# Layer norms kept in PSUM, other PSUM banks for three projections and four turns, small steps and transfers spread, in a two-network transformer kernel

## The reference, cut to what matters

```python
for l in range(DEPTH):                       # first network, block1
    x = x + 0.5 * swiglu(rmsnorm(x, ffn1_norm[l]), w_ffn1_in[l], w_ffn1_out[l])
    u = rmsnorm(x, mix_norm[l])
    # three branches: latent attention (c_q, c_kv), a gated recurrence whose lower bounds
    # come from a softmax over hg_lower_bounds, and attention to a memory (w_mem_kv)
    x = x + merged @ w_out[l]
    x = x + 0.5 * swiglu(rmsnorm(x, ffn2_norm[l]), w_ffn2_in[l], w_ffn2_out[l])
x = rmsnorm(x, final_norm)
for l in range(DEPTH):                       # second network, block2
    x = _layer_norm(DN_ALPHA * x + 0.5 * _swiglu(x, ffn1_w1[l], ffn1_w2[l]), ln1_g[l], ln1_b[l])
    mix = _token_mix(x, w_in[l], ...)        # branches nsa (with a bias table), swa, fox
    x = _layer_norm(DN_ALPHA * x + mix, ln2_g[l], ln2_b[l])
    x = _layer_norm(DN_ALPHA * x + 0.5 * _swiglu(x, ffn2_w1[l], ffn2_w2[l]), ln3_g[l], ln3_b[l])

def _layer_norm(x, g, b):
    mu = mean(x); var = mean(square(x - mu))
    return (x - mu) * rsqrt(var + LN_EPS) * g + b
```

## Time and profile before

| | |
|---|---|
| median of three runs | 2748.06 us (2747.74 to 2748.56) |
| the profiled execution | 2751.27 us, of it 2749.5 us from the first to the last instruction |
| granted clock of TensorE, mean | 0.994 |
| PE, PEld busy | 98%, 90% |
| DVE, ACT, POOL busy | 31%, 47%, 74% |
| DMA | 474.66 MB, 173 GB/s on average |

### The profile page before, as it was taken

One profiled execution on the slowest core, in us unless ns is written; L12 is line 12 of the kernel. 1 busy time (PEld: TensorE's weight loads), 2 busy tenths in 40 slices (PEclk: granted clock), 3 DMA queues, 4 the chain that ended last, 5 costly groups with the idle time before them and its releaser, 6 DMA issues. The chain is left out here.

```text
span 2749.5 us, 46223 instructions
## 1 busy us (share of the span) xinstructions
PE 2695.5 (98%) x18758; PEld 2483.4 (90%) x18758; DVE 856.2 (31%) x1483; ACT 1283.7 (47%) x1868; POOL 2038.7 (74%) x906
## 2 busy tenths in 40 slices
PE   8999999999999999999999999999999999999998
PEld 6999899899898989989989899998988989999798
DVE  2543354111225245321211323632131132263212
ACT  4454555444444455444444444644444443464443
POOL 7888466888887845788798774368879877436886
PEclk9999999999999999999999999999999999999999
DMA  6556534555665543755565554245546555424554
GB/s 231 184 192 204 172 116 135 194 185 177 213 191 175 196 158 115 184 184 186 175 210 184 173 177 158 85 162 183 185 168 211 188 172 177 148 88 157 184 187 142
DMA packets 128731, 474.66 MB, mean 173 GB/s; under 512 B 14432, under 2 KB 14432, under 8 KB 127520
## 3 DMA queue, kind: packets, MB, share of 16 engines
q1 hardware_dynamic: 124704, 454.09, 49.5%
q0 software_dynamic: 3840, 17.81, 2.3%
HBM read 469.22 MB, written 2.62 MB: 172 GB/s over the span
## 5 line engine op out<-in xcount | busy, mean ns | idle before, releaser
L1021 POOL TENSOR_TENSOR rest<-ring,upper 128x1024 fp32r<-128x1024 f32 (+1 forms) x834 | 1998.8, 2416 | 648.2 <-ACT upper L1799 629.2
L1799 ACT ACTIVATE upper<-ring 128x1024 fp32r<-128x1024 f32 (+1 forms) x834 | 869.0, 1053 | 784.3 <-DMA ring<-in_weights 783.5
L372 PE MATMUL psA<-xT_upper,upper 128*128 128x256 f32 x2832 | 395.8, 282 | 4.5 <-DVE Sc L1695 2.4
L372 PE MATMUL psA<-xT_rest,upper 128*128 128x256 f32 x2832 | 397.4, 283 | 0.0
L372 PE MATMUL psA<-xT_upper,rest 128*128 128x256 f32 x2832 | 390.1, 280 | 0.0
L372 PEld LDWEIGHTS psA<-xT_upper,upper 128*128 128x128 f32 x2832 | 370.0, 189 | 18.8 <-ACT arena L1799 3.5
L372 PEld LDWEIGHTS psA<-xT_rest,upper 128*128 128x128 f32 x2832 | 365.3, 192 | 0.0
L1261 DVE TENSOR_TENSOR psA<-sil,psA 128x256 f32<-128x256 f32 x144 | 61.8, 429 | 958.8 <-ACT sil L1799 958.8
L372 PEld LDWEIGHTS psA<-xT_upper,rest 128*128 128x128 f32 x2832 | 358.7, 189 | 0.0
L372 PE MATMUL psY<-upper,hT_upper 128*128 128x512 f32 x704 | 204.7, 396 | 3.4 <-DVE hT_rest L1263 3.4
L372 PE MATMUL psY<-upper,hT_rest 128*128 128x512 f32 x704 | 205.8, 397 | 0.0
(11 more groups left out here) (264 smaller groups left out, 3194.1 us busy)
## 6 DMA issues: line engine op xcount, KB each, us to landing
ring<-in_weights SPq DMA_DIRECT2D x862, 512.0 KB, 3.4
G<-in_rows POOLq DMA_DIRECT2D x6, 1024.0 KB, 7.7
G<-in_rows POOLq DMA_DIRECT2D x7, 512.0 KB, 6.2
arena<-rel_by_distance POOLq DMA_DIRECT2D x8, 256.0 KB, 11.9
x<-in_x SPq DMA_DIRECT2D x2, 512.0 KB, 5.9
par<-in_params POOLq DMA_DIRECT2D x4, 256.0 KB, 6.0
xn<-in_mem POOLq DMA_DIRECT2D x1, 1024.0 KB, 10.8
memory_transposed<-arena POOLq DMA_DIRECT2D x1, 1024.0 KB, 5.7
```

Source lines behind the costliest of these rows:

```text
L372: i = pe.matmul(out, lhsT, rhs, start=start, stop=stop)
L1021: pool.tensor_tensor(rest[:, r, 0:n], ring[:, r, 0:n], upper[:, r, 0:n], ALU.subtract)\
L1799: act.activation(out, in_, func, **kw).then_inc(*up)
```

## The change

- **Layer norms in PSUM.** The half sums plus `x` stay in the Y bank instead of going to `x`; ACT squares the two banks one after the other (two operations of 512 for one of 1024); DVE subtracts the mean and multiplies by the gain in place, bank by bank, each behind ACT's square of it; the two sums of squares are added by a new small `tensor_tensor`; the last operation reads the bank and writes `x`. A Y bank is given back only then. POOL no longer waits for `x` between its power and its splits.
- **Banks.** `mk` goes to Y0 and Y1; the latents of tile 1 turn into Y0 and Y1; `kc vc` and `kb` go to Y1. `vf` of tile 0 is copied before the splits up to piece 72.
- **Bounds.** The ten operations of step 15 are spread over steps 11, 13, 15, 17 and 18 (two each) and the last one goes from 18 to 21; ACT's exponential goes from step 14 to 7 and its logarithm from 17 to 20.
- **Bias transfers.** After each second one of the eight POOL splits one piece.

```diff
+        def scaled(norm, tt, h):
+            return taken(("y", norm, 2 * tt + h)) if is_layer_norm(norm) else sig["scaled"].after(("norm", norm, tt, h))
...
-                by_features("mk", 2, rhs=memory_parts)
+                by_features("mk", 2, rhs=memory_parts, into=["Y0", "Y1"])
...
-                    turn("T0", ("cT", t, 0), [cn[:, t, j * P:(j + 1) * P] for j in range(3)])
-                    turn("T1", ("cT", t, 1), [cn[:, t, j * P:(j + 1) * P] for j in range(3, 5)])
+                    turn("TY"[t] + "0", ("cT", t, 0), [cn[:, t, j * P:(j + 1) * P] for j in range(3)])
+                    turn("TY"[t] + "1", ("cT", t, 1), [cn[:, t, j * P:(j + 1) * P] for j in range(3, 5)])
...
-                by_features("kc vc", 1)
+                by_features("kc vc", 1, into=["Y1"])
...
-                by_parts(fill(pe, next_a(), lab)[:, 0:S], s, filled(lab))
+                by_parts(fill(pe, "Y1", lab)[:, 0:S], s, filled(lab))
...
                     norm_power(norm, tt)
-                    for h in range(2):
-                        pool.wait_ge(*sig["scaled"].after(("norm", norm, tt, h)))
+                    if not is_layer_norm(norm):
+                        for h in range(2):
+                            pool.wait_ge(*scaled(norm, tt, h))
...
-                    for p in range(0, P, COPIES):
+                    for n, p in enumerate(range(0, P, COPIES)):
                         pool.dma_start(BIAS[p:p + COPIES], ...
+                        if n % 2:
+                            upto(after_mix() - MERGED + 1 + n // 2)
...
-                    add_sums(norm, tt)
-                    for b in (2 * tt, 2 * tt + 1):
-                        dve.wait_ge(*taken(("y", norm, b)))
+                    for h in range(2):
+                        lab = ("y", norm, 2 * tt + h)
+                        dve.wait_ge(*full(lab))
+                        stt_(at(lab), at(lab), 0.5, x[:, tt, 512 * h:512 * h + 512], ALU.mult, ALU.add,
+                             accum_out=st[:, 20 + 2 * tt + h:21 + 2 * tt + h]).then_inc(*sig["residual added"].up(lab))
+                    dve.wait_ge(*sig["residual added"].after(("y", norm, 2 * tt + 1)))
...
+                    def gained(h):
+                        y = at(("y", norm, 2 * tt + h))
+                        dve.wait_ge(*sig["square sum"].after(("norm", norm, tt, h)))
+                        stt_(y, y, st[:, 26 + tt:27 + tt], lnr[:, 0, 512 * h:512 * h + 512], ALU.add, ALU.mult)\
+                            .then_inc(*sig["vector step"].up())
...
-                    stt_(xn[:, tt, :], x[:, tt, :], st[:, 26 + tt:27 + tt], lnr[:, 0, :], ALU.add, ALU.mult)\
-                        .then_inc(*sig["vector step"].up())
-                    dve.wait_ge(*sig["square sum"].after(("norm", norm, tt)))
-                    ts_(st[:, tt:tt + 1], st[:, 16 + 2 * tt:17 + 2 * tt], 1.0 / D, 1e-5, ALU.mult, ALU.add)\
+                    gained(0)
+                    dve.wait_ge(*sig["square sum"].after(("norm", norm, tt, 1)))
+                    link(tt_(st[:, tt:tt + 1], st[:, 16 + 2 * tt:17 + 2 * tt], st[:, 17 + 2 * tt:18 + 2 * tt], ALU.add))
+                    ts_(st[:, tt:tt + 1], st[:, tt:tt + 1], 1.0 / D, 1e-5, ALU.mult, ALU.add)\
                         .then_inc(*sig["variance"].up(("norm", norm, tt)))
+                    gained(1)
...
-                        stt_(x[:, tt, c], xn[:, tt, c], st[:, 8 + tt:9 + tt], lnr[:, 1, c], ALU.mult, ALU.add)\
-                            .then_inc(*sig["scaled"].up(("norm", norm, tt, h)))
+                        stt_(x[:, tt, c], at(lab), st[:, 8 + tt:9 + tt], lnr[:, 1, c], ALU.mult, ALU.add)\
+                            .then_inc(*read(lab))
...
-                also = {5: lambda: bounds(l, 0), 15: lambda: bounds(l, 1), 18: lambda: bounds(l, 2)}
+                also = {5: lambda: bounds(l, 0), 11: lambda: bounds(l, 1), 13: lambda: bounds(l, 2), 15: lambda: bounds(l, 3),
+                        17: lambda: bounds(l, 4), 18: lambda: bounds(l, 5), 21: lambda: bounds(l, 6)}
...
-                    act.activation(other_junk[:, tt, :], x[:, tt, :], ACT.Square, bias=st[:, 26 + tt:27 + tt],
-                                   accum_out=st[:, 16 + 2 * tt:17 + 2 * tt]).then_inc(*sig["square sum"].up(("norm", norm, tt)))
+                    for h in range(2):
+                        act.activation(other_junk[:, tt, 512 * h:512 * h + 512], at(("y", norm, 2 * tt + h)), ACT.Square,
+                                       bias=st[:, 26 + tt:27 + tt], accum_out=st[:, 16 + 2 * tt + h:17 + 2 * tt + h])\
+                            .then_inc(*sig["square sum"].up(("norm", norm, tt, h)))
...
-                also = {14: lambda: bounds(0), 17: lambda: bounds(1)}
+                also = {7: lambda: bounds(0), 20: lambda: bounds(1)}
...
-                for t in range(TT):
-                    copy(("vf", t), VF[:, t, :], piece=69)
+                copy(("vf", 0), VF[:, 0, :])
+                copy(("vf", 1), VF[:, 1, :], piece=69)
```

More of the change, by code:

```diff
@@ L434, in turn_half @@
                     turn(f"T{h}", ("norm", norm, tt, h), [src[:, tt, (4 * h + q) * P:(4 * h + q + 1) * P] for q in range(4)],
-                         sig["scaled"].after(("norm", norm, tt, h)))
+                         scaled(norm, tt, h))
             def wait_half(norm, tt):
@@ L508, in features, with by_features @@
                                filled(lab) if j == 1 and k == kt - 1 else None)
-            def by_features(label, banks, rhs=None):
+            def by_features(label, banks, rhs=None, into=None):
                 rhs = xT if rhs is None else rhs
@@ L514, in by_features @@
                     lab = (label, n)
-                    out = fill(pe, next_a(), lab)
+                    out = fill(pe, into[n] if into else next_a(), lab)
                     for j in range(2):
@@ L752, in block1 @@
                     pe.wait_ge(*taken(("c", 2 + t)))
-                    turn("T0", ("cT", t, 0), [cn[:, t, j * P:(j + 1) * P] for j in range(3)])
-                    turn("T1", ("cT", t, 1), [cn[:, t, j * P:(j + 1) * P] for j in range(3, 5)])
+                    turn("TY"[t] + "0", ("cT", t, 0), [cn[:, t, j * P:(j + 1) * P] for j in range(3)])
+                    turn("TY"[t] + "1", ("cT", t, 1), [cn[:, t, j * P:(j + 1) * P] for j in range(3, 5)])
                 gate(range(4))
-                for h in range(2):
-                    pe.wait_ge(*taken(("cT", 1, h)))
+                for t in range(TT):
+                    for h in range(2):
+                        pe.wait_ge(*taken(("cT", t, h)))
                 for n in range(4):
@@ L983, in _ @@
                 for h in range(2):
-                    sp.wait_ge(*sig["scaled"].after(("norm", 3 * LAYERS, tt, h)))
+                    sp.wait_ge(*scaled(3 * LAYERS, tt, h))
                 sp.dma_start(a["out"].rearrange("(t p) d -> p t d", p=P)[:, tt, :], x[:, tt, :])\
@@ L1043, in next_rows @@
                 for h in range(2):
-                    pool.wait_ge(*sig["scaled"].after(("norm", norm, 1, h)))
+                    pool.wait_ge(*scaled(norm, 1, h))
                 load_rows(norm + 1)
@@ L1462, in bounds @@
                     link(dve.reciprocal(s4, s4))
+                elif step == 2:
                     link(tt_(e[:, 0:4], e[:, 0:4], s4, ALU.mult))
                     link(tt_(e[:, 4:8], e[:, 4:8], s4, ALU.mult))
+                elif step == 3:
                     link(tt_(lb, e[:, 0:4], e[:, 4:8], ALU.add))
                     link(tt_(lb, lb, e[:, 0:4], ALU.subtract))
+                elif step == 4:
                     link(ts_(lb, lb, par[:, 46:47], None, ALU.mult))
                     link(ts_(oml, lb, -1.0, 1.0, ALU.mult, ALU.add))
+                elif step == 5:
                     link(ts_(zero, lbt[:, 16:24], 0.0, NEG, ALU.is_equal, ALU.mult))
@@ L2042, in block1 @@
                 gate_out([2, 3])
-                for b in range(TT):
-                    act.wait_ge(*taken(("c", b)))
+                for h in range(2):
+                    act.wait_ge(*taken(("cT", 1, h)))
                 act.wait_ge(*sig["sums made"].after(0))
@@ L2054, in block1 @@
                         for h in range(2):
-                            act.wait_ge(*taken(("cT", 1, h)))
+                            act.wait_ge(*taken(("cT", 0, h)))
                     else:
```

3 lines of the change are left out of this document (1 added, 2 removed).

## The result

The changed kernel takes 2726.36 us (median of four runs, 2723.69 to 2726.82); the kernel before took 2748.04 us beside it (four runs, 2747.74 to 2748.56). The ratio is 0.9922, with an interval of 0.9909 to 0.9935. A second set of six runs of it, beside the experiments, gave 2725.14 us and a ratio of 0.9916 (0.9902 to 0.9931). The forecast was 2722.0, with a range of 2715 to 2736. Between the two profiled spans (2749.5 and 2724.8 us) lie 24.6 us; the sum made on that profile was 26.1. Against a second profile of the kernel before (experiment 11, span 2737.9 us) the changed one is only 13.1 us shorter, so these 24.6 us are a difference of two executions, and not yet the worth of the change.

The account below looks back on a forecast made before the run. PE, busy 98% of the span, was taken to bound the kernel. Banks 10.1, bounds 5.0, bias transfers 1.7 and norms 9.3 sum to 26.1 us; taken off the median 2748.06 this gives 2722 us, range 2715 to 2736.

Parts of the forecast that it names:

- Banks: PE's waits for banks at mk/mv, latent turns, qa, qb and vt go: 10.1 us.
- The rival that the ring takes the banks' place: At qa, qb and vt PE may meet the weights' ring instead of the bank: +3.5 us; no separate chance.
- Bounds: Layer 1: a stall of 3.58 us and 1.39 us of slow down matmuls go, 5.0 us; layer 0 gains nothing.
- Bias transfers: Spread by pairs between POOL's splits, they let weight loads in between: 1.7 us, or 0 if the queue only moves later.
- Norms: Norms 7, 9, 10 gain 2.2 us net, norms 8 and 11 gain 7.8, norm 12 loses 0.7: 9.3 us.
- one stall of three: Norms 8 and 11, stalls of 1.42, 1.84 and 0.64 us idle: first shortened, second gone, third mostly staying.
- the hold-up of tile 0: Norms 8 and 11, first stall: without DVE's hold-up in tile 0, 0.75 of the 1.58 us stays.
- the clock's 1.1 us: Norms 8 and 11: slow transposes and matmuls behind the old stalls, 1.1 us in each, expected to go.
- tile 0's path: DVE's path in each norm tile becomes 0.37 us longer, paid at tile 0 of norms 7, 9, 10 and in norm 12.
- The held add: Rival: the norms' new two-SBUF-input add is held beside POOL in all 12 tiles, 26.3 us lost, 2757.6 us; chance 0.03.
- The 0.9 us: Norms: the skill's VectorE cycle table adds 0.13 us in each of seven exposed tiles; by the profile rows nothing.
- Re-formed stalls: Rival: PE, arriving earlier, waits for splits or loads instead; gain 15.6 us, 2732 us; chance 0.26, shared with idle norms.

Follow-up runs that it names:

- experiment 11: The kernel before, unchanged, run and profiled a second time: 2744.87 us (twelve runs), profiled span 2737.9 us.
- no_bounds: The changed kernel with ten bounds operations in step 15 again: 2727.01 us, ratio 0.9931; second set 2730.57 us, ratio 0.9935.
- only_bounds: The kernel before with the bounds spread and nothing else: 2743.93 us (eleven runs), ratio 0.9991 (0.9981 to 1.0001).
- old_norms_free_pool: The changed kernel with the old layer norms, but POOL not waiting for x: 2741.53 us (twelve runs), ratio 0.998.
- pool_waits: The changed kernel with POOL again waiting for x between its power and its splits: 2727.2 us, ratio 0.9931.
- before_again: The kernel before, unchanged, the same run as experiment 11: 2744.87 us (twelve runs).
- no_norms: The changed kernel with the old layer norms and POOL's old wait for x: 2731.96 us, ratio 0.9941.
- the pointer add: The changed kernel with the new add of two sums as a tensor_scalar with a pointer scalar: 2725.26 us, ratio 0.9925.
- experiments 11 and 12: Repeats with second profiles: the kernel before, unchanged, 2744.87 us; the changed kernel with the old bounds, 2730.57 us.

## Why the prediction was right

**Banks: right.** The sum was 10.1 us; the places show 10.9, and without the banks the median is 8.7 us higher. The rival that the ring takes the banks' place at `qa`, `qb` and `vt` did not come: 7.5 us there against the 6.9 of the sum.

**Bounds: right on the profile, too large as a term.** The prediction had 5.0 us in layer 1, and the two profiles differ by 4.97 there. But the stall is in two of four executions. Eleven runs of no_bounds have a median of 2730.2, 4.2 us over the changed kernel (1.0 in the first set, 5.4 in the second), and only_bounds gives 3.9, not clear of noise. The step that failed is that the stall's whole price was taken off the median. Price times frequency, by four profiles, is an estimate of 5.0 x 2/4 = 2.5 us; the timed runs say 3.9 to 4.2. How often the stall occurs is known only roughly.

**Bias transfers: mis-sized, and the mechanism not shown.** 1.7 us summed, 1.4 between the two profiles, 0.74 in the mean of all profiles, and nothing in the median when they are undone. The transfers land a median of 8.0 us after their issue where it was 11.9, so they queue less behind one another. That the weights' loads get in between is not shown: ACT's wait for weights ahead of the merge was 4.11 us and is 6.47.

**Norms: the mechanism right, one stall of three taken for certain.** That operations with one PSUM input are not held beside POOL is shown by L1239's 747 to 762 ns and by old_norms_free_pool, where the old forms without POOL's wait lose 9.6 us. That the wait's removal is worth 1.4 us in each of norms 8 and 11 is shown by pool_waits. The places give 9.6 us net, the sum had 9.3. Without the norm edits the median is only 5.9 us higher. Norms 8 and 11 were priced at 7.8 us together; at the places they cost 9.0 us over the changed kernel in the profile of before, 7.8 in only_bounds, 6.2 in before_again and 4.6 in no_norms. Two things in them come and go. One is the hold-up of tile 0, in the first two profiles alone, which the sum priced at 2 x 0.83 us. The other is the granted clock: behind the second and third stall, in which PE stands idle for 1.9 and 0.6 us within 3.3, it falls to half (1.2 GHz) in five of these eight norms, and in none of the eighteen of the nine profiles with the changed norms. A norm with neither cost 1.8 or 1.9 us, with one of them 2.7 to 4.4, with both 4.4 to 4.9. Windows of norm 11 behind the stalls, before, before_again, and the changed kernel at the same matmuls:

```profile
2556.00:2560.00 4.00, 3.54 (x13) 2.97 (x14) 2.67 (x5) 2.13 (x4) 0.00 (x0) 0.57 0.00 0
```

```profile
2544.00:2548.00 4.00, 4.00 (x13) 3.16 (x12) 2.56 (x4) 3.14 (x5) 0.85 (x1) 0.50 0.00 0
```

```profile
2532.00:2536.00 4.00, 3.88 (x20) 2.95 (x21) 3.01 (x4) 3.31 (x5) 1.10 (x1) 1.00 0.00 0
```

The third number from the right is the granted clock, of which 0.50 is 1.2 of 2.4 GHz. The prediction took the clock's 1.1 us in each of the two norms as certain to go; they went, and they were not always there. Inside the term, tile 0's path from the mean to its last operation is 0.48 us longer where 0.37 was worked out, and the end 0.96 where it was 0.7. ACT's square of a bank takes 0.68 us, not 0.63, and the first in-place operation starts 0.95 us behind the mean, not 0.80. The accumulator's read behind a sum that goes to PSUM takes 142 ns (83 behind the old sum, in no_norms) and costs nothing here: from the first half sum to the start of the mean it is 1.50 us in the changed kernel and 1.51 before.

**The held add: the rival's mechanism was real, and small.** Five of the twelve adds were held, to at most 1.79 us, under the 1.9 from which it would have decided. Three of the five are in norms 7, 9 and 10, where the prediction had POOL's pieces over by then; PE did not wait there. It waited for the other two, idle 0.4 us each, and the pointer add gives 0.3 of each back. The Trainium skill (SBUF — State Buffer, "Who interferes with whom") has two SBUF inputs as one condition, and an operation in a 2-port perf mode, which a copy or a `tensor_scalar` with one SBUF input can enter, as another; the prediction named the first alone. By that rule, the trace agrees with the first: the same sum as a `tensor_scalar` of one column, whose second number comes as a scalar, is never above 206 ns. It shows too that one SBUF input is no safe sign: `tensor_scalar` operations of 4 and 8 columns are held up to 2.41 and 2.27 us in experiments 11 and 12, where 0.17 is what they take alone, and a copy of 128x256 in SBUF took 2.38 us where the next took 0.28.

**No extra cost of PSUM.** DVE's last pass takes 1.41 us for its two halves with the bank as an input, and took 1.41 with `xn`. The 0.9 us worked out in the prediction from the Trainium skill's errata table (VectorE: DVE Perf Modes) is not there; no run here shows its 65 ns.

**Re-formed stalls: two small ones.** The wait on L1444 in layer 0 cost 1.0 us and the RMS norm 0.9. Both are again POOL over DVE or ahead of it: two copies of the rotation beside its splits took 2.39 and 2.38 us and ended late, and the power of the RMS norm began only when a pair of splits was over. The first is in six of the fourteen profiles, with the bounds spread and without, so it is not an effect of that edit. None of the three profiles of the kernel before and only_bounds has it, so it may still be one of the change as a whole.

**From 2722 to 2726.** That the sum of 26.1 us came so near the 24.6 between the first two profiles is in part luck, as the 13.1 us against the second profile show. The sum was taken from an execution of 2751.3 us. Over all 65 timed runs of the kernel before, the mean is 2747.1 and the range 2739.7 to 2755.4; the profile used had the stall of layer 1, the held tiles 0 and one of the slow stretches below, each of which some other executions lack. A median gives back less than such a profile shows. The removals add to 5.9 + 8.7 + 4.2 - 0.5 = 18.3 us, the whole change to 2747.5 - 2726.0 = 21.5 us (medians of 65 and of ten runs). Medians of five runs, in kernels that spread over 1 to 8 us, may hide the 3.2 us between; what they are is not settled. One sum of the prediction does not come out: its lower bound counts 5.5 us, and the parts it names (0.37 us five times, and rests of 0.75 and 0.7 us twice) add to 4.8. Nothing hangs on it.

## What to carry to other kernels

Where POOL works beside DVE, look at each DVE operation for two SBUF inputs: give wide ones a PSUM input, and a sum of single columns a scalar operand, and the waits that keep POOL away can go. Then look in the trace whether what is left is really free, since copies and `tensor_scalar` operations of some columns were held here as well. A small operation behind a busy POOL can take 2.3 us as a wide one takes 3.3; spread a row of ten. A stall that hangs on where another engine's run of work happens to end must be priced by how often it occurs: profile the kernel before twice, and take what both executions show as certain and the rest as a share.

## What had not been expected of the hardware

The same program on one chip lies at 2740.1 us in one run and at 2755.4 in another (23 runs in one set). Most of the difference between two profiles of it (11.6 us, of two sets) stands at a few places: 5.0 us at the bounds of layer 1, 1.5 and 1.7 at the held tiles 0, and stretches with a low granted clock, 3.0 us at the compressed attention of the second layer and 1.5 the other way in norm 11. The changed kernel has such stretches too, at the first matmuls of compressed attention. Windows of the kernel before, then of the changed one (us, PE, PEld, DVE, ACT, POOL busy, granted clock, DMA share, GB/s):

```profile
1688.00:1692.00 4.00, 4.00 (x26) 4.00 (x26) 2.03 (x8) 0.96 (x3) 0.00 (x0) 0.66 0.02 4
```

```profile
1676.00:1680.00 4.00, 4.00 (x20) 4.00 (x20) 1.49 (x6) 0.30 (x1) 0.00 (x0) 0.50 0.03 11
1680.00:1684.00 4.00, 4.00 (x25) 3.87 (x25) 0.54 (x3) 1.25 (x2) 2.03 (x1) 0.67 0.00 0
```

PE is shown busy in them throughout, behind a short wait for DVE. In the changed kernel the first has 0.50 of the clock (1.2 of 2.4 GHz), where the stretch ahead had 0.98; a share between, as 0.66, is a mean of both levels. The edits do not touch this place, and it moves the time of an execution by some 1.5 us either way: in layer 0 the changed kernel's profile is 1.6 us slower there than that of before, in layer 1 it is 1.5 us faster.
